# A decoder step on one core: both exponentials of a head pair in one slot, attention's later steps moved behind them, two buffers for the values

## The reference, cut to what matters

```
s = einsum('nhpd,pkd->nhpk', qh, sub_keys);  sv, si = top_k(s, 16)
...  fv, fpos = top_k(cand, 16);  gate = softmax(fv)
act = gelu(einsum('nd,nhkd->nhk', x, u_tab[eidx]))
out = einsum('nhk,nhkd->nd', gate * act, v_tab[eidx])
```

```
logits = einsum(q, k) * hd ** -0.5 + bias
p = exp(logits - max);  den = sum(p);  o = einsum(p, v) / den
x = x + gate1 * (concat(hA, rmsnorm(att)) @ w_out)
h2 = rmsnorm(x) * (1 + scale2) + shift2
```

## Times and profile before

| what | value |
|---|---|
| median of 3 runs | 3994.39 us (3993.17, 3994.39, 13917.62) |
| profiled execution | 3981.78 us, span 3980.0 us |
| busy share of the span | PE 78%, DVE 60%, ACT 39%, POOL 32% |
| granted TensorE clock, mean | 0.839 |
| gather issues (L1219) | 1088 |
| table loads at L1528 | 80 of 1283 ns |
| HBM traffic | 1365 MB read, 94 MB written, 367 GB/s over the span |

### The profile page before, as it was taken

One profiled execution on the slowest core, in us unless ns is written; L12 is line 12 of the kernel. 1 busy time (PEld: TensorE's weight loads), 2 busy tenths in 40 slices (PEclk: granted clock), 3 DMA queues, 4 the chain that ended last, 5 costly groups with the idle time before them and its releaser, 6 DMA issues.

```text
span 3980.0 us, 46682 instructions
## 1 busy us (share of the span) xinstructions
PE 3103.8 (78%) x16448; PEld 1371.4 (34%) x16448; DVE 2403.3 (60%) x5612; ACT 1570.8 (39%) x4397; POOL 1278.6 (32%) x1202
## 2 busy tenths in 40 slices
PE   6699999596787778678777867877787788767777
PEld 1466565454223224123323423342332333214111
DVE  1355544237569558756955774596569447848744
ACT  0233332232543453364345335434533453333333
POOL 0000000022444344444433443443344334444432
PEclk9899999597788689689968977896788789778689
DMA  9773536764999999999999999999999999999998
GB/s 380 285 245 123 195 124 52 294 222 166 412 402 397 415 411 399 404 410 402 400 409 380 400 400 373 393 403 417 371 397 399 403 371 395 404 380 400 417 414 364
DMA packets 238950, 1395.82 MB, mean 351 GB/s; under 512 B 41812, under 2 KB 68308, under 8 KB 92020
## 3 DMA queue, kind: packets, MB, share of 16 engines
q0 software_dynamic: 168480, 1198.61, 75.1%
q1 hardware_dynamic: 65224, 173.65, 13.4%
q10 hardware_dynamic: 5012, 20.58, 1.3%
HBM read 1365.02 MB, written 94.27 MB: 367 GB/s over the span
## 4 chain that ended last, share of the span: by engine, by line
DMA 27%; PE 23%; DVE 20%; ACT 8%; issue 2%; POOL 1%; ACTq 0%; SPq 0%; POOLq 0%; DVEq 0%
DMA mem<-in_experts,mem 24%; PE psum L1421 10%; DVE mem L1744 10%; PE psum L1299 3%; DVE mem L1589 3%; DVE mem L1588 3%; DMA mem<-qkv_rows 2%; PE psum L1274 2%; PE psum L1327 2%; ACT L1528 1%; DVE mem L1591 1%; ACT mem L1532 1%; ACT mem L1529 1%; PE psum L1260 1%; PE psum L1228 1%
## 5 line engine op out<-in xcount | busy, mean ns | idle before, releaser
L1421 PE MATMUL psum<-mem 64*64 64x512 f32 x8192 | 1392.2, 772 | 657.6 <-ACT mem L1532 656.0
L1744 DVE CUSTOM_DVE_ANT_0 mem<-mem 128x1024 f32<-128x1024 f32 x1088 | 1324.6, 1221 | 771.3 <-DMA mem<-in_experts,mem 761.6
L1219 POOL DMA_INDIRECT mem<-in_experts,mem x1088 | 1213.8, 1116 | 1772.0 <-PE psum L1421 1606.7
L1528 ACT ACTIVATE mem<-mem 128x1 f32<-128x1 f32 x1088 | 219.2, 201 | 1501.3 <-DVE mem L1744 1500.0
L1421 PEld LDWEIGHTS psum<-mem 64*64 64x64 f32 x8192 | 269.3, 159 | 1410.7 <-ACT mem L1532 1214.5
L1532 ACT ACTIVATE mem<-mem 128x64 f32<-128x64 f32 x1088 | 379.1, 348 | 35.6
L628 PE MATMUL psum<-mem 128*128 128x512 f32 (+3 forms) x864 | 339.0, 544 | 11.0 <-ACT mem L588 9.8
L1529 ACT ACTIVATE mem<-mem 128x1 f32<-128x1 f32 x1088 | 320.4, 294 | 35.3
L1327 PEld LDWEIGHTS psum<-mem 128*128 128x128 f32 x2304 | 286.9, 203 | 100.7 <-issue 93.6
L1327 PE MATMUL psum<-mem 128*128 128x128 f32 (+1 forms) x2304 | 312.2, 291 | 3.3 <-ACT mem L1479 3.0
L628 PEld LDWEIGHTS psum<-mem 128*128 128x128 f32 (+1 forms) x864 | 147.4, 188 | 176.2 <-issue 162.4
(11 more groups left out here) (266 smaller groups left out, 2747.8 us busy)
## 6 DMA issues: line engine op xcount, KB each, us to landing
out_k_s<-in_cache_k SPq DMA_DIRECT2D x8, 4080.0 KB, 17.6
out_v_s<-in_cache_v SPq DMA_DIRECT2D x8, 4080.0 KB, 29.6
mem<-in_w_ada SPq DMA_DIRECT2D x12, 2048.0 KB, 15.2
mem<-in_experts,mem POOLq DMA_INDIRECT x1088, 10.4
mem<-in_vals POOLq DMA_DIRECT2D x16, 1024.0 KB, 7.8
mem<-in_keys_t POOLq DMA_DIRECT2D x14, 1024.0 KB, 6.0
mem<-in_x SPq DMA_DIRECT2D x16, 512.0 KB, 14.8
mem<-in_w_in ACTq DMA_DIRECT2D x2, 3072.0 KB, 25.4
```

The lines of the kernel that those rows point to most:

```text
L1219: pool.indirect_dma_start(out=ring[:, g % N_SLOTS].rearrange("p a n -> p (a n)"), out_offset=None, in_=ins["experts"][:, :], in_offset=bas ...
L1421: mm = nc.tensor.matmul(psum[(LOW, HIGH)[half], tok.start // HALF_P], diag[tok, g % 4], ring[tok, g % N_SLOTS, 1, cols], start=c == 0, sto ...
L1528: chain.link(a.activation(weight[:, c:c + 1], dots[:, c:c + 1], ACT.Gelu))
L1744: v.tensor_tensor_reduce(row, row, h2[i % 2], 1.0, 0.0, ALU.mult, ALU.add, dots[:, c:c + 1]).then_inc(sig["dots"], 1)
```

## The change

The table `slots` puts the exponentials of heads 2j and 2j + 1 in the same pick (11, 19, 27, 35), and the later steps of the heads four picks apart from each other: transposes at 13, 17, 21, 25, 29, 33, 37, 41, their copies 2 picks later, the products with the values 3 picks later, the divisions 5 picks later. The scores and the bias steps stay where they were. All that follows attention stands 5 picks later; the search has its 16 lists from pick 78 on, the first half of the indices at pick 119, the second half and `gates` at pick 125.

The values of a pair have two buffers, by turns. The second one is `mod_a`, which held the modulation rows; these now lie as 32 rows of 128 in a piece of their own, so that spreading a row of 512 takes four matmuls of 128 columns in place of one. `vals_in` of pair 1 is issued with the first loads of the tile, that of pairs 2 and 3 once the products of the pair before the last are done. In the second part the order of SP's loads changes too.

```diff
     if n < NT:
         at["head"] = [at["load"] + 3 + 8 * (hh // 2) + 3 * (hh % 2) for hh in range(H_B)]
-        at["rms"] = at["head"][-1] + 9
+        at["exp"] = [first + (6, 3)[hh % 2] for hh, first in enumerate(at["head"])]
+        at["probs"] = [first + (8, 9)[hh % 2] for hh, first in enumerate(at["head"])]
+        at["copy"] = [first + 2 for first in at["probs"]]
+        at["values"] = [first + 3 for first in at["probs"]]
+        at["heads"] = [first + 5 for first in at["probs"]]
+        at["rms"] = at["heads"][-1]
...
-    at["q"] = [first + j * min(45, 99 - first) // 15 for j in range(2 * HEADS)]
+    at["q"] = [first + j * min(45, 103 - first) // 15 for j in range(2 * HEADS)]
...
-    p_rows = mod_a[0:4]
+    p_rows = work.take(P)[0:4 * KD]
...
-    vals = heads.take(NT, P)
+    vals = (heads.take(NT, P), mod_a.rearrange("p (t e) -> p t e", t=NT))
...
         def vals_in(n, j):
-            if j >= 1:
-                sp.wait_ge(sig["o_ps"], H_B * n + 2 * j)
+            if j >= 2:
+                sp.wait_ge(sig["o_ps"], H_B * n + 2 * (j - 1))
...
             bias_in(n, 2)
+            if n >= 1:
+                vals_in(n, 1)
...
             bias_in(n, 3)
+            if n >= 1:
+                keys_in(n, 2)
             bias_in(n, 4)
             if n >= 1:
-                vals_in(n, 1)
-                keys_in(n, 2)
+                vals_in(n, 2)
             bias_in(n, 5)
+            if n >= 1:
+                keys_in(n, 3)
             bias_in(n, 6)
             if n >= 1:
-                vals_in(n, 2)
-                keys_in(n, 3)
+                vals_in(n, 3)
             bias_in(n, 7)
-            if n >= 1:
-                vals_in(n, 3)
...
         def spread_row(row, half, bank):
-            return nc.tensor.matmul(psum[:, bank], ident[0:4, row:row + 1].broadcast_to((4, P)), p_rows[:, half * 512:(half + 1) * 512], start=True, stop=True)
+            for q in range(4):
+                part = row * KD + half * 4 + q
+                mm = nc.tensor.matmul(psum[:, bank, q * P:(q + 1) * P], ident[0:4 * KD, part:part + 1].broadcast_to((4 * KD, P)), p_rows, start=True, stop=True)
+            return mm
...
-                if c == first + 4:
+                if c == at["probs"][hh]:
...
-                if c == first + 7:
+                if c == at["values"][hh]:
...
-                if c == first + 3:
+                if c == at["exp"][hh]:
...
-                if c == first + 6:
+                if c == at["copy"][hh]:
...
-                if c == first + 9:
+                if c == at["heads"][hh]:
```

More of the change, by code:

```diff
@@ L955, in stage3 @@
     diag = work.take(4, HALF_P)
-    work.take(4, HALF_P)
-    front_end = work.at + PICKS
+    front_end = work.at + 3 * P
     x1_odd = work.take(D)
@@ L1003, in stage3 @@
     s_out = s_picked.take(H_B // 2, HD)
-    s_att = (s_ring.take(HD), x1_odd[:, PICKS:PICKS + HD])
+    s_att = (s_ring.take(HD), x1_odd[:, 3 * P:3 * P + HD])
     s_gain = idx_even.bitcast(F32)[:, HALF:HALF + HD]
@@ L1053, in _ @@
         sp.dma_start(s_bias, scratch["s_bias"].ap()).then_inc(sig["s_bias_in"], 16)
-        sp.dma_start(p_rows, scratch["mod"].ap()[0:1, 2 * D:].rearrange("o (r d) -> (o r) d", d=D)).then_inc(sig["p_rows_in"], 16)
+        sp.dma_start(p_rows, scratch["mod"].ap()[0:1, 2 * D:].rearrange("o (r d) -> (o r) d", d=P)).then_inc(sig["p_rows_in"], 16)
         def bias_in(n, hh):
@@ L1071, in vals_in @@
         def vals_in(n, j):
-            if j >= 1:
-                sp.wait_ge(sig["o_ps"], H_B * n + 2 * j)
+            if j >= 2:
+                sp.wait_ge(sig["o_ps"], H_B * n + 2 * (j - 1))
             src = scratch["qkv"].ap()[0:(n + 1) * P, 2 * W_B + j * P:2 * W_B + (j + 1) * P]
-            sp.dma_start(vals[:, 0:n + 1], src.rearrange("(t p) e -> p t e", p=P)).then_inc(sig["vals_in"], 16)
+            sp.dma_start(vals[j % 2][:, 0:n + 1], src.rearrange("(t p) e -> p t e", p=P)).then_inc(sig[f"vals_in{j % 2}"], 16)
         def attention_first(n):
@@ L1082, in attention_first @@
             if n == 0:
-                sp.dma_start(vals[:, 0:4].rearrange("p j e -> p (j e)"), scratch["qkv"].ap()[rows_at(n), 2 * W_B:]).then_inc(sig["vals_in"], 16)
+                sp.dma_start(vals[0][:, 0:4].rearrange("p j e -> p (j e)"), scratch["qkv"].ap()[rows_at(n), 2 * W_B:]).then_inc(sig["vals_in0"], 16)
             bias_in(n, 0)
@@ L1268, in attention @@
                     if n == 0 and hh == 0:
-                        pe.wait_ge(sig["vals_in"], 16)
+                        pe.wait_ge(sig["vals_in0"], 16)
                     if n >= 1 and hh % 2 == 0:
-                        pe.wait_ge(sig["vals_in"], 16 * (4 * (n - 1) + j + 2))
+                        pe.wait_ge(sig[f"vals_in{j % 2}"], 16 * (2 * (n - 1) + j // 2 + 1 + (j % 2 == 0)))
                     for t in range(n + 1):
-                        some = vals[:, t if n >= 1 else j, half]
+                        some = vals[j % 2][:, t, half] if n >= 1 else vals[0][:, j, half]
                         mm = nc.tensor.matmul(psum[:, 6 + hh % 2, 0:HD], probs_t[:, t], some, start=t == 0, stop=t == n)
```

## The result

The changed kernel took **4057.11 us** (median of 4 runs, 4046.89 to 4058.05) beside 3999.53 us for the kernel before on the same chip (4 runs, 3993.17 to 13917.62): ratio **1.0136**, 95% interval 1.0119 to 1.0154, slower by about 55 us. The ratio is of fast runs alone, so the one of 13917.62 us has no part in it, and it is not exactly the quotient of the two medians. My forecast was 3990 with a range of 3955 to 4030. What came is the rival "slower by a new wait", and more than its full price (4043). The profiled execution has a span of 4054.9 us, 75 more than before; some 15 us of these 75 are there because the profiled execution of the kernel before (3981.78 us) was one of its shortest.

What follows compares the result with a forecast made beforehand. The DMA engines were taken as the bound, with 43 us lost in picks 8 to 39 of rounds 1 to 7. Terms -25 + 23 - 2 = -4 us took the median from 3994.4 to 3990, range 3955 to 4030.

Steps and rivals of the forecast that it cites:

- slower by a new wait: Scores of head 2, pick 13, rounds 5 to 7: keys later than 11.4 us cover; 4005, in full 4043; chance 0.18.
- Bound: Picks 8 to 39, rounds 1 to 7: DMA engines set the time, losing 43 us against 420 GB/s.
- The 43 us: Time lost in picks 8 to 39 of rounds 1 to 7 by running under 420 GB/s.
- Table loads and waits, -25: Rounds 4 to 7: fewer table loads and shorter DVE and ACT waits give back 25 us; bounds 0 and 43.
- Two exponentials in one pick, nothing: Pick 11: ACT held 5 us against 3.7, first user at pick 13, covered by gathers in flight; no cost.
- The new order on q1, how late: Old keys of pair 1, rounds 2 to 7: late behind pair 1's values and a later `gates`, 58 us in all.
- Its price, +23: Late loads on q1: 19 us beyond what gathers in flight cover, 4 us for biases; bounds 0 and 76.
- First window, -2: Before the first gather: search steps move behind the sample row on DVE, 2 us saved; bounds -5 and +2.
- Rows spread by four matmuls, nothing: Spreading modulation rows: 64 calls at 0.04 us more each, +0, or 3 us if none hides.

Runs made afterwards that it cites:

- linear_before: The kernel before with Copy in place of Gelu, which needs no table loads (the output differs): 1.0029 of the kernel before.
- buffers_only: The changed kernel's two value buffers and order on q1, with all steps at their places of before: 1.0009 of the kernel before.
- keys_first: The changed kernel with the old keys of pair 1 ahead of the values of pair 1 on q1: 1.0047 of the kernel before.
- two_fixes: The changed kernel with pair 1's old keys ahead of its values on q1, and copies and products one pick earlier: 0.9985 of the kernel before.
- first_window: The changed kernel with the places of before for tile 0 alone: 1.0145 of the kernel before.
- late_search: The kernel before with all that follows attention 5 picks later and the search 1 pick denser: 1.0004 of the kernel before.
- late_division: keys_first with the divisions on DVE two picks later, save the last: 1.0053 of the kernel before.
- whole_values_after: The changed kernel with values also written, and read, as runs of (n + 1) x 512 bytes a partition: 1.0034 of the kernel before.
- products_early: whole_values_after with copies and products with the values one pick earlier, ahead of ACT's burst: 0.9875 of the kernel before.

## Why the prediction was wrong, step by step

- **Bound.** Right: the DMA engines set these stretches, and what they lose by late issues is what can be won. The 43 us were the right size.
- **Table loads and waits, -25.** This step failed. For the loads, I took their share of the chain in round 7, 16.6%, for time that would come back; linear_before shows that none of it does. I also called ACT "never most of one" stretch, where the earlier trace rows have it busy for 56 to 63% of each. For the waits, only ACT's for the transposes went (88.9 to 12.2 us). DVE's for the products I had put down to late values, with "about two picks" from their issue to the products; the table has five, and in round 6 it was 13.6 us. PE waited only 16.2 us for values; 68 of DVE's 89.0 us stood behind ACT's pick, and buffers_only, with both buffers at the old places, still has 99.6. With the keys mended, picks 8 to 39 took 708.6 us against 685.9, and the whole kernel 1.0047. By these two executions the term was +23, not -25; by the timed runs keys_first is 19 us above, its later start included.
- **Two exponentials in one pick, nothing.** This is where most of that came from: two_fixes takes 20 us of it back. I compared 5 us of ACT with 3.7 and named pick 13 as their first user. I did not ask what of PE stands behind the gather sum that waits for them: the products of the head before, at the next pick, and the division two picks on. With the copy it is 6.0 us, PE stops 5.7, DVE up to 10.4.
- **The new order on q1, how late.** Right in place and in the sum, and the sum in part by luck. I had 1.4, 3.7, 5.9, 16.2, 18.4 and 12.7 us for rounds 2 to 7, 58 in all; PE stood 3.7, 6.8, 10.8, 11.7, 11.4 and 11.0, 55.4 in all. In rounds 5 to 7 the stops are up to 7 us shorter than I said, in rounds 2 to 4 up to 5 us longer, and the errors cancel. The 8 us of pause that I took over to rounds 2 to 4 was too much. I had also left out that SP's own issues would stall.
- **Its price, +23.** Mis-sized: keys_first gives back 47 us in the profile and 0.9%, 36 us, in the runs. I let the gathers in flight pay for the first 11.4 us of every stop and 2 us for the restart. The DMA engines did run on for some 10 us in round 6, but the stop emptied them, and the way back to full cost 9 us. Nor was 11.4 us always in flight: in round 3 a stop of 6.8 us emptied them too (16 GB/s and less from 1743 to 1746 us). I had applied a cover to a wait without asking what happens at its end. Picks 8 to 15 of rounds 2 to 7 grew by 2.5, 5.6, 10.1, 9.1, 10.4 and 11.0 us, 49 us, near the 55.4 us of the stops; so the nearest price was their own length.
- **First window, -2.** Wrong sign in the trace: the first gather was issued at 986.45 in place of 973.74. The places moved for tile 0 as well, and no gather there covers that; with them put back it is issued at 974.8 (first_window). The search alone moves the first dot by only 3.7 us (late_search).
- **Rows spread by four matmuls, nothing.** Outside picks 8 to 39, where they stand, rounds 1 to 7 took 1796.5 us in all, 1798.9 before. A call is four matmuls in place of one, so rows 10 give 0.02 us a call and not 0.04; it changes nothing.
- **The rivals.** The right one had 0.18. Its place was that of the trace, but its point of decision (11.4 us) and its price used the same cover. It held one mechanism; the second, ACT's burst, stood in my sum at nothing. That the result lies 14 us beyond this rival's full price fits the 20 us that the earlier products took back in two_fixes.

## What to carry to other kernels

A share of the chain of waits is not a saving: take the work out in a trial, or show that a stretch with it runs below the rate that its bound allows. When several instructions are put in one slot, list for every engine what waits behind the burst, one and two engines on, and put the dependent step ahead of it. A load that must be early goes ahead of loads in many small pieces on the same queue, and a stop that drains a gather pipeline costs its refill and not only its excess over what is in flight. A wait that falls to nothing is no gain by itself: in late_division and linear_before others grew in its place.

## What the runs showed that I had not expected

- SP's issuing instruction itself stalled in rounds 6 and 7 from about the fifth load on that stood outstanding on q1: in round 7 12.5 us for two and 21.9 us for one, where an issue otherwise takes 0.3 to 0.4.
- Two delays of the same loads, harmless one by one (1.0009 and 1.0004), are both there in the kernel that gets 0.9% back once one of them is taken out (1.0136 to 1.0047).
- Values in runs of 512 (n + 1) bytes in place of 512 make the changed kernel 1.0% faster and the kernel before 0.4%, with the same bytes.
- With PE standing some 5 us in each eighth pick, the granted clock was 0.66 to 0.71 over the last 94 us of that stretch of round 7 (whole_values_after); with the same work and shorter stops it was 1.00 and 0.86 over 67 us (products_early).
